# One core, one transformer layer with a mixture of experts: the last expert's products in banks of their own, weighted in halves, and the final norms of both tiles interleaved

## The chip, the cores and the metric

The kernel runs on one NeuronCore of a Trainium2 chip. TensorE (PE) multiplies, VectorE (DVE), ScalarE (ACT) and GpSimd (POOL) do the rest, SyncE (SP) issues the transfers. The metric is the device time of one launch in microseconds; lower is better. Each engine works through its own list of instructions in order, and the lists are tied together by semaphores that the kernel sets and waits for by name.

## The reference, cut to what matters

A first block (attention and a convolutional feed-forward part) and a second block (gated linear attention, pooling, and a mixture of 32 experts) run over 256 tokens of width 1024. The change lies in the end of the second block: the last expert, the sum over experts, and the last norm.

```python
def expert_block(args):
    xb, e = args
    return (jax.nn.silu(xb @ w_gate[e]) * (xb @ w_up[e])) @ w_down[e]
...
y_rows = y_rows * row_w[:, None].astype(y_rows.dtype)
out = jnp.zeros((T + 1, D), y_rows.dtype).at[row_token].add(y_rows)[:T]
...
x = x + hier_moe(h2, ...)
return rmsnorm_2(x, norm_f_g)      # x * rsqrt(mean(x*x) + eps) * g
```

All data are fp32, 256 tokens are two tiles of 128, an expert has an inner width of 256.

## The kernel before, in words

Weights come in 165 units of 1 MB (128 partitions by 2048 numbers), through a ring of 6 slots in SBUF; SP issues a unit as soon as `unit_used` says that its slot is free. The experts are worked on one after another, each with up to 64 tokens (`CH`); what does not fit in 64 goes to a second pass behind `If(total > 0)`, which the inputs here do not need. TensorE's list is skewed: in the turn of expert e (`experts(e)`) stand the gate and up products of expert e+1, the two transposes of expert e's activations (`expert_turn`, L1039), the scattering of expert e-1 (`scatter`, L1053) and the down products of expert e (`expert_down`, L1047).

- Down products: 4 fp32 products of 128x512 into banks 2 and 3 of PSUM (`psum[:, 2 + n, :]`), where every expert's stand. Each is two instructions in the trace, so there are 8 of them in a row. Their end adds 1 to `unit_used`.
- Weighting: ACT (`results`, L1421) waits for the down products, reads both banks (128x1024), multiplies each row by its routing weight and writes the rounded high part into `YH` (the tile `weighted`), `y_hi`. DVE (`results`: `tokens_of`, L2027, then `low_results`, L2031) writes for 64 partitions the rest that the rounding left, `y_lo`.
- Scattering: 4 products of 128x512 multiply `YH` by a 0/1 matrix (`W`, the tile `token_onehot`) and add into banks 4 to 7, two banks for each tile of tokens.
- The copy of the transposes: ACT's `turned` (L1164, 128x256) reads bank 1 and writes `AE`, which the down products read (`ae_ready`).

For the last expert (31) the turn has no products of a next one, so its order on TensorE is: transposes of 31, scattering of 30, down products of 31, and behind the turn the scattering of 31, which adds 1 to `y_done` for each tile. ACT does `results(30)`, `turned(31)`, `results(31)`.

The final norm goes tile by tile. DVE adds the tile's two banks to `X` (L2119, `final_x`); ACT squares and sums (L1145); DVE adds epsilon (L1566, 128x1); POOL takes the power -0.5 (L1499, 128x1); DVE multiplies `X` by the root and by the gain row `final` (L2124) and writes `HN`; SP stores the tile (L483). DVE's list holds all of tile 0 before any of tile 1:

```python
for tt in range(TT):
    dve.wait_ge(y_done, tt + 1)
    tt_op(X[:, tt, :], X[:, tt, :], psum[...], ADD).then_inc(final_x, 1)
    add_eps(11 + tt)
    roots_ready(11 + tt)
    dve.wait_ge(final_x, tt + 1)
    stt(HN[:, tt, :], X[:, tt, :], rstd[...], r_("final"), MUL, MUL).then_inc(out_ready, 1)
```

Between the last expert and the final norm each engine loads the number `total` and branches around the second pass.

Of the kernel before, what the change touches and what calls it, by code (L numbers as in the profile page):

```python
# [18 lines left out]
P = 128  # L19
S = 256  # L20
TT = S // P
# [34 lines left out]

NORM_PARTS = (2, 4, 2, 2, 2, 2, 2, 2, 2, 8, 2, 1, 1)
WHOLE = (2, 3, 4)
GROUP_SPANS = {2: slice(0, 512), 3: slice(512, 768), 4: slice(768, 1024)}


# [81 lines left out]
def build(nc, x_in, units_in, const_in, vec_in, rows_in, small_in, bias_in, out):  # L143
# [8 lines left out]
    with ctx:  # L152
# [3 lines left out]
        def sem(name):  # L156
            return ctx.enter_context(nc.semaphore(name))
# [161 lines left out]
        with nc.sbuf_tensor("tables_ahead", [P, A.at], fp32):  # L319
# [57 lines left out]
                  "more_lo", "more_scattered"))  # L377
        more_in, more_table, more_table_sb, more_added = map(
            sem, ("more_in", "more_table", "more_table_sb", "more_added"))
        out_ready, out_stored, final_x = sem("out_ready"), sem("out_stored"), sem("final_x")  # L380
        up_conv, pool_zero = sem("up_conv"), sem("pool_zero")
        dve_steps, act_steps, pool_steps = sem("dve_steps"), sem("act_steps"), sem("pool_steps")

# [61 lines left out]
        def _(sp):  # L445
# [32 lines left out]
                                     .rearrange("a p n -> p (a n)")).then_inc(more_loaded, 16)  # L478
                sp.nop()
            sp.nop()  # L480
            for tt in range(TT):
                sp.wait_ge(out_ready, tt + 1)
                sp.dma_start(out[tt], HN[:, tt, :]).then_inc(out_stored, 16)  # L483
            sp.wait_ge(out_stored, 16 * TT)


# [1 line left out]
        def _(pe):  # L488
# [575 lines left out]
            def experts(e, i=0):  # L1064

                if e < EXPERTS - 1:
                    pe.wait_ge(xw_lo, i * 2 + (e + 2))
                    pe.wait_ge(up_summed, i * 2 + (e + 1))
                    expert_up(0, XW[:, (e + 1) % 2], parts(gate_of(e + 1), i)).then_inc(unit_used, 1)
                    w = parts(gate_of(e + 1) + 1, i)  # L1070
                pe.wait_ge(at_ready, i * 2 + (e + 1))
                if e < EXPERTS - 1:
                    expert_up(1, XW[:, (e + 1) % 2], w, range(1))
                expert_turn().then_inc(at_tr, 1)
                if e < EXPERTS - 1:
                    expert_up(1, XW[:, (e + 1) % 2], w, range(1, KD)).then_inc(unit_used, 1)
                if e >= 1:
                    pe.wait_ge(y_lo, i * 2 + e)
                    for tt in range(TT):
                        last = scatter((e - 1) % 2, tt, 4 + 2 * tt, first=e == 1)  # L1080
                    last.then_inc(scattered, 1)
                w = unit(pe, down_of(e), i)
                pe.wait_ge(ae_ready, i * 2 + (e + 1))
                expert_down(w).then_inc(unit_used, 1)
# [9 lines left out]
                experts(4, i)  # L1094
                experts(5, i)
            experts(EXPERTS - 2)
            experts(EXPERTS - 1)
            pe.wait_ge(y_lo, EXPERTS)
            for tt in range(TT):
                scatter((EXPERTS - 1) % 2, tt, 4 + 2 * tt, final=True).then_inc(y_done, 1)  # L1100

            pe.wait_ge(total_ready, 1)
            total = pe.value_load(totali[0:1, 0:1], min_val=0, max_val=TASKS)
# [26 lines left out]
        def _(act):  # L1130
# [329 lines left out]
                experts(4, i)  # L1460
                experts(5, i)
            experts(EXPERTS - 2)
            experts(EXPERTS - 1)
            results(EXPERTS - 1)

            act.wait_ge(total_ready, 1)
            total = act.value_load(totali[0:1, 0:1], min_val=0, max_val=TASKS)
# [13 lines left out]
            act.nop()  # L1481
            for tt in range(TT):
                act.wait_ge(final_x, tt + 1)
                mean_squares(11 + tt, [X[:, tt, :]])


        @block.gpsimd
# [69 lines left out]
        def _(dve):  # L1557
# [517 lines left out]
                experts(4, i)  # L2075
                experts(5, i)
            experts(EXPERTS - 2)
            experts(EXPERTS - 1)
            results(EXPERTS - 1)

            dve.wait_ge(total_ready, 1)
            total = dve.value_load(totali[0:1, 0:1], min_val=0, max_val=TASKS)
# [34 lines left out]
            for tt in range(TT):  # L2117
                dve.wait_ge(y_done, tt + 1)
                tt_op(X[:, tt, :], X[:, tt, :], psum[:, 4 + 2 * tt:6 + 2 * tt, :].rearrange("p a b -> p (a b)"), ADD  # L2119
                      ).then_inc(final_x, 1)  # L2120
                add_eps(11 + tt)
                roots_ready(11 + tt)
                dve.wait_ge(final_x, tt + 1)
                stt(HN[:, tt, :], X[:, tt, :], rstd[:, 11 + tt, 0:1], r_("final"), MUL, MUL).then_inc(out_ready, 1)  # L2124


def constants():
# [136 lines left out]
```

## Time and profile before

| what | value |
|---|---|
| time, median of 3 runs | 869.8 us (869.47 to 870.5) |
| the profiled execution's own time | 868.98 us |
| its span, first to last instruction | 867.2 us |
| PE busy | 813.8 us, 94% of the span |
| DVE, ACT, POOL busy | 523.7, 451.1, 125.7 us |
| mean granted TensorE clock | 0.970 of full speed |
| moved by DMA | 181.44 MB, mean 209 GB/s |

The busy shares are means over the whole kernel. The change touches the last 25 us only, and there the slices of the page read 8 and 3 tenths for PE: TensorE is not what the end waits for. What matters is the chain of waits from the down products of the last but one expert to the last store.

### The profile page before, as it was taken

To read this page: it belongs to the slowest core of one execution; us is meant where nothing else is said; L and a number is where in the kernel's file an instruction comes from. 1 tells how busy PE (TensorE), PEld (TensorE's weight loads), DVE (VectorE), ACT (ScalarE), POOL (GpSimd) and SP (SyncE) were. 2 spreads that over 40 slices of the span, in tenths; PEclk is the share of its full clock that TensorE was granted. 3 is DMA by queue.
4 is the path that set the end of the run, shared out by engine and by line. 5 is a ranking of instruction groups with operands and counts; after the bars stand their busy time and mean duration, and the time that the engine had idled before them with its cause. 6 is when DMAs were issued, how large, how long until landed. Compare 5 with 4: busy or idle time off the path is not lost.

```text
span 867.2 us, 13148 instructions
## 1 busy us (share of the span) xinstructions
PE 813.8 (94%) x4792; PEld 660.9 (76%) x4792; DVE 523.7 (60%) x657; ACT 451.1 (52%) x590; POOL 125.7 (14%) x94
## 2 busy tenths in 40 slices
PE   6999999999999996998999989779999999999983
PEld 5888755999999994697899976467777777777761
DVE  3244435466556564655155565858888888888863
ACT  3243444454455443463244444267777777777741
POOL 0000001323422433103000000011111111111100
PEclk9999999999999998998799999889999999999996
DMA  9922221455555553152154543059999999999931
GB/s 368 386 98 97 97 97 48 150 192 194 193 172 179 185 190 103 43 190 102 50 195 146 194 149 143 0 197 351 369 353 378 373 352 353 380 359 373 373 146 50
DMA packets 25090, 181.44 MB, mean 209 GB/s; under 512 B 2784, under 2 KB 3040, under 8 KB 3296
## 3 DMA queue, kind: packets, MB, share of 16 engines
q1 hardware_dynamic: 25056, 180.97, 56.3%
q8 instruction: 24, 0.39, 0.2%
q14 instruction: 10, 0.08, 0.0%
HBM read 179.91 MB, written 1.05 MB: 209 GB/s over the span
## 4 chain that ended last, share of the span: by engine, by line
PE 86%; DVE 6%; ACT 3%; POOL 2%; issue 1%; DMA 1%; POOLq 0%; ACTq 0%; SPq 0%; DVEq 0%
PE psum L823 36%; PE psum L1032 15%; PE psum L1047 13%; PE psum L519 4%; PE psum L1053 3%; PE psum L618 3%; PE psum L527 2%; PE psum L577 1%; ACT junk L1145 1%; PE psum L1039 1%; PE psum L1024 1%; PE psum L942 1%; DVE arena L1764 1%; DVE ffn_w_low L438 1%; PE psum L940 1%
## 5 line engine op out<-in xcount | busy, mean ns | idle before, releaser
L438 DVE TENSOR_TENSOR ffn_w_low<-ring,ffn_w_high 128x2048 fp32r<-128x2048 f32 x57 | 135.0, 2372 | 123.4 <-ACT ffn_w_high L433 123.3
L433 ACT ACTIVATE ffn_w_high<-ring 128x2048 fp32r<-128x2048 f32 x57 | 109.2, 1918 | 144.1 <-PE psum L823 143.8
L823 PE MATMUL psum<-ht_high,ffn_w_high 128*128 128x256 f32 x576 | 164.3, 285 | 1.7 <-DVE ffn_w_low L438 1.1
L823 PE MATMUL psum<-ht_low,ffn_w_high 128*128 128x256 f32 x576 | 163.5, 284 | 0.0
L823 PE MATMUL psum<-ht_high,ffn_w_low 128*128 128x256 f32 x576 | 163.5, 284 | 0.0
L438 DVE TENSOR_TENSOR expert_w_low<-ring,expert_w_high 128x2048 fp32r<-128x2048 f32 x48 | 110.0, 2292 | 20.3 <-ACT expert_w_high L433 19.9
L1047 PE MATMUL psum<-ring,arena 128*128 128x512 f32 x256 | 116.7, 599 | 0.0
L823 PEld LDWEIGHTS psum<-ht_high,ffn_w_high 128*128 128x128 f32 x576 | 111.1, 193 | 3.2 <-issue 1.4
L1032 PE MATMUL psum<-expert_w_high,xw 128*128 128x256 f32 x384 | 106.1, 311 | 5.8 <-POOL xw L1543 3.9
L823 PEld LDWEIGHTS psum<-ht_low,ffn_w_high 128*128 128x128 f32 x576 | 111.1, 193 | 0.3
L823 PEld LDWEIGHTS psum<-ht_high,ffn_w_low 128*128 128x128 f32 x576 | 111.0, 193 | 0.0
L1032 PE MATMUL psum<-expert_w_low,xw 128*128 128x256 f32 x384 | 96.4, 286 | 0.0
L433 ACT ACTIVATE expert_w_high<-ring 128x2048 fp32r<-128x2048 f32 x48 | 91.4, 1904 | 3.5 <-PE psum L823 3.5
L1047 PEld LDWEIGHTS psum<-ring,arena 128*128 128x128 f32 x256 | 49.0, 192 | 49.8 <-issue 47.1
L1032 PEld LDWEIGHTS psum<-expert_w_high,xw 128*128 128x128 f32 x384 | 74.6, 194 | 12.3 <-POOL xw L1543 4.3
L1032 PEld LDWEIGHTS psum<-expert_w_low,xw 128*128 128x128 f32 x384 | 74.6, 194 | 3.6 <-issue 3.6
L1543 POOL TENSOR_TENSOR xw<-arena,xw 128x512 fp32r<-128x512 f32 x32 | 38.4, 1201 | 255.9 <-ACT xw L1164 255.9
L1164 ACT ACTIVATE arena<-psum 64x512 f32<-64x512 f32 (+6 forms) x96 | 46.2, 486 | 44.4 <-PE psum L1032 18.9
L1421 ACT ACTIVATE weighted<-psum,arena 128x1024 fp32r<-128x1024 f32 x32 | 35.8, 1119 | 59.1 <-PE psum L1047 59.1
L1499 POOL TENSOR_TENSOR rstd<-ms,neghalf 128x1 f32<-128x1 f32 (+3 forms) x19 | 14.1, 744 | 305.7 <-DVE ms L1566 305.7
L2031 DVE SCALAR_TENSOR_TENSOR weighted<-psum,arena,weighted 64x1024 fp32r<-64x1024 f32 x32 | 41.3, 1291 | 23.0 <-ACT weighted L1421 22.9
L1510 POOL TENSOR_TENSOR arena<-arena 128x512 f32<-128x512 f32 x11 | 31.9, 2901 | 127.2 <-ACT arena L1308 119.4
(296 smaller groups left out, 1405.4 us busy)
## 6 DMA issues: line engine op xcount, KB each, us to landing
ring<-units_in SPq DMA_DIRECT2D x165, 1024.0 KB, 5.9
rows<-rows_in SPq DMA_DIRECT2D x1, 1688.0 KB, 12.3
arena<-bias_in SPq DMA_DIRECT2D x1, 1536.0 KB, 15.6
small<-small_in SPq DMA_DIRECT2D x1, 1232.0 KB, 25.5
const<-const_in SPq DMA_DIRECT2D x1, 1073.0 KB, 23.0
X<-x_in SPq DMA_DIRECT2D x1, 1024.0 KB, 4.9
out<-HN SPq DMA_DIRECT2D x2, 512.0 KB, 2.6
vec<-vec_in SPq DMA_DIRECT2D x1, 113.5 KB, 4.4
```

Source lines behind the costliest of these rows:

```text
L433: nc.scalar.activation(parts_slot(n)[0], w, ACT.Copy).then_inc(hi_ready, 1)
L438: nc.vector.tensor_tensor(l, ring[:, n % RING, :], h.bitcast(fp32), SUB).then_inc(lo_ready, 1)
L519: last = mm(psum[:, bank, half * S:half * S + S], w[:, k * FF_CHUNK + half * P:k * FF_CHUNK + half * P + P], HT[:, k, :], start=k == 0, st ...
L618: last = mm(psum[:, 4 + 2 * tt + n, :], MIXT[:, 2 * j + kk, tt * P:(tt + 1) * P], w[:, kk * D + n * 512:kk * D + n * 512 + 512], start=j = ...
L823: last = mm(o, l[a], r[b], start=start and (a, b) == pairs[0], stop=stop and (a, b) == pairs[-1])
L1032: last = mm(psum[:, 0, g * D_EXP:(g + 1) * D_EXP], x[:, k, :], part[:, k * D_EXP:(k + 1) * D_EXP], start=k == 0 and part is w[0], stop=k = ...
L1047: last = mm(psum[:, 2 + n, :], AE[:, f, :], w[:, a:a + 512], start=f == 0, stop=f == 1)
L1164: return nc.scalar.activation(out_, in_, ACT.Copy)
L1421: return nc.scalar.activation(YH[:, par, :], psum[:, 2:4, :].rearrange("p a b -> p (a b)"), ACT.Copy, scale=TW[:, ds(weight, 1)])
L1510: nc.gpsimd.tensor_tensor(AF[:, c % 2], G[:, c % 2], up, MUL).then_inc(af_parts, 1)
L1543: nc.gpsimd.tensor_tensor(XW[:, e % 2, :, CH:], XS[:, :, ds(at, CH)], XW[:, e % 2, :, 0:CH].bitcast(fp32), SUB).then_inc(xw_lo, 1)
L2031: return stt(y, psum[CH:P, 2:4, :].rearrange("p a b -> p (a b)"), TW[CH:P, ds(column + EXPERTS, 1)], y.bitcast(fp32), MUL, SUB)
```

## The change

The last expert's turn is written out apart from `experts(e)` on the three engines.

- TensorE: down products of 31 go to banks 0 and 1 and stand right behind the transposes of 31, ahead of the scattering of 30. Each bank has a signal of its own (`last_down`). The scattering of 31 goes half by half: both tiles' products of columns 0 to 511, then both tiles' of columns 512 to 1023.
- ACT: `turned(31)` stands ahead of `results(30)`; the weighting of 31 is two instructions of 128x512 (`last_hi`) in place of one of 128x1024.
- DVE: the rest of 31 is two instructions of 64x512 (`last_lo`).
- Final norms: DVE adds both tiles first, then adds epsilon for tile 0, multiplies tile 1 by the gain row without its root (`gained`), adds epsilon for tile 1, and finishes tile 0 as before. ACT multiplies tile 1 by its root.

```diff
@@ TensorE
             experts(EXPERTS - 2)
-            experts(EXPERTS - 1)
-            pe.wait_ge(y_lo, EXPERTS)
+            last_e = EXPERTS - 1
+            pe.wait_ge(at_ready, EXPERTS)
+            expert_turn().then_inc(at_tr, 1)
+            w = unit(pe, down_of(last_e))
+            pe.wait_ge(ae_ready, EXPERTS)
+            for n in range(2):
+                for f in range(2):
+                    a = f * D + n * 512
+                    last = mm(psum[:, n, :], AE[:, f, :], w[:, a:a + 512], start=f == 0, stop=f == 1)
+                last.then_inc(last_down, 1)
+            pe.wait_ge(y_lo, EXPERTS - 1)
             for tt in range(TT):
-                scatter((EXPERTS - 1) % 2, tt, 4 + 2 * tt, final=True).then_inc(y_done, 1)
+                last = scatter((last_e - 1) % 2, tt, 4 + 2 * tt)
+            last.then_inc(scattered, 1)
+            for n in range(2):
+                pe.wait_ge(last_lo, n + 1)
+                for tt in range(TT):
+                    last = mm(psum[:, 4 + 2 * tt + n, :], W[:, last_e % 2, tt * P:(tt + 1) * P],
+                              YH[:, last_e % 2, n * 512:(n + 1) * 512], start=False, stop=True)
+                    if n == 1:
+                        last.then_inc(y_done, 1)
+            pe.nop().then_inc(unit_used, 1)
@@ ScalarE
-            experts(EXPERTS - 1)
-            results(EXPERTS - 1)
+            turned(EXPERTS - 1)
+            results(EXPERTS - 2)
+            act.wait_ge(scattered, EXPERTS - 2)
+            for n in range(2):
+                act.wait_ge(last_down, n + 1)
+                nc.scalar.activation(YH[:, (EXPERTS - 1) % 2, n * 512:(n + 1) * 512], psum[:, n, :], ACT.Copy,
+                                     scale=TW[:, 2 * EXPERTS - 1:2 * EXPERTS]).then_inc(last_hi, 1)
...
             for tt in range(TT):
                 act.wait_ge(final_x, tt + 1)
-                mean_squares(11 + tt, [X[:, tt, :]])
+                mean_squares(FINAL + tt, [X[:, tt, :]])
+            act.wait_ge(gained, 1)
+            act.wait_ge(rstd_ready, roots_before(FINAL + 2))
+            nc.scalar.activation(HN[:, 1, :], HN[:, 1, :], ACT.Copy, scale=rstd[:, FINAL + 1, 0:1]).then_inc(out_second, 1)
@@ VectorE
-            experts(EXPERTS - 1)
-            results(EXPERTS - 1)
+            results(EXPERTS - 2)
+            dve.wait_ge(scattered, EXPERTS - 2)
+            tokens_of((EXPERTS - 1) % 2, EXPERTS - 1)
+            for n in range(2):
+                dve.wait_ge(last_hi, n + 1)
+                y = YH[CH:P, (EXPERTS - 1) % 2, n * 512:(n + 1) * 512]
+                stt(y, psum[CH:P, n, :], TW[CH:P, 2 * EXPERTS - 1:2 * EXPERTS], y.bitcast(fp32), MUL, SUB
+                    ).then_inc(last_lo, 1)
...
-                add_eps(11 + tt)
-                roots_ready(11 + tt)
-                dve.wait_ge(final_x, tt + 1)
-                stt(HN[:, tt, :], X[:, tt, :], rstd[:, 11 + tt, 0:1], r_("final"), MUL, MUL).then_inc(out_ready, 1)
+            add_eps(FINAL)
+            dve.wait_ge(final_x, 2)
+            tt_op(HN[:, 1, :], X[:, 1, :], r_("final"), MUL).then_inc(gained, 1)
+            add_eps(FINAL + 1)
+            roots_ready(FINAL)
+            stt(HN[:, 0, :], X[:, 0, :], rstd[:, FINAL, 0:1], r_("final"), MUL, MUL).then_inc(out_first, 1)
```

SP waits for `out_first` and then for `out_second` in place of two counts of `out_ready`.

TensorE's list before, from the down products of expert 30 to the scattering of 31 (`ring` holds the down weights, `arena` the activations, `weighted` is `YH`):

```order
L1047 MATMUL psum<-ring,arena 128x512 [waits ae_ready,unit_loaded1]
L1047 MATMUL psum<-ring,arena 128x512 x3
L1039 MATMUL psum<-const,arena 128x64 [waits at_ready]
L1039 MATMUL psum<-const,arena 128x64
L1053 MATMUL psum<-weighted,token_onehot 128x512 [waits y_lo]
L1053 MATMUL psum<-weighted,token_onehot 128x512 x3
L1047 MATMUL psum<-ring,arena 128x512 [waits ae_ready,unit_loaded2]
L1047 MATMUL psum<-ring,arena 128x512 x3
L1053 MATMUL psum<-weighted,token_onehot 128x512 [waits y_lo]
L1053 MATMUL psum<-weighted,token_onehot 128x512 x3
```

The same place in the list of the changed kernel (its lines are numbered anew; L1051 and L1109 are the down products of 30 and of 31, L1057 and L1118 the scattering of 30 and of 31):

```order
L1051 MATMUL psum<-ring,arena 128x512 [waits ae_ready,unit_loaded1]
L1051 MATMUL psum<-ring,arena 128x512 x3
L1043 MATMUL psum<-const,arena 128x64 [waits at_ready]
L1043 MATMUL psum<-const,arena 128x64
L1109 MATMUL psum<-ring,arena 128x512 [waits ae_ready,unit_loaded2]
L1109 MATMUL psum<-ring,arena 128x512 x3
L1057 MATMUL psum<-weighted,token_onehot 128x512 [waits y_lo]
L1057 MATMUL psum<-weighted,token_onehot 128x512 x3
L1118 MATMUL psum<-weighted,token_onehot 128x512 [waits last_lo]
L1118 MATMUL psum<-weighted,token_onehot 128x512
L1118 MATMUL psum<-weighted,token_onehot 128x512 [waits last_lo]
L1118 MATMUL psum<-weighted,token_onehot 128x512
```

The down products of 31 moved ahead of the wait for `y_lo`, and the last scattering has two waits.

VectorE's list before, in the final norm, behind the branch:

```order
L2119 TENSOR_TENSOR X<-X,psum 128x1024 [waits y_done]
L1566 TENSOR_SCALAR ms<-ms 128x1 [waits squares_summed]
L2124 SCALAR_TENSOR_TENSOR HN<-X,rstd,rows 128x1024 [waits final_x,rstd_ready]
L2119 TENSOR_TENSOR X<-X,psum 128x1024 [waits y_done]
L1566 TENSOR_SCALAR ms<-ms 128x1 [waits squares_summed]
L2124 SCALAR_TENSOR_TENSOR HN<-X,rstd,rows 128x1024 [waits final_x,rstd_ready]
```

The same place after (`rows` is the tile of the gain row; L2159 is tile 1 by its gain, L2162 tile 0 by root and gain):

```order
L2155 TENSOR_TENSOR X<-X,psum 128x1024 [waits y_done] x2
L1596 TENSOR_SCALAR ms<-ms 128x1 [waits squares_summed]
L2159 TENSOR_TENSOR HN<-X,rows 128x1024 [waits final_x]
L1596 TENSOR_SCALAR ms<-ms 128x1 [waits squares_summed]
L2162 SCALAR_TENSOR_TENSOR HN<-X,rstd,rows 128x1024 [waits rstd_ready]
```

The second addition moved to the front, and a product of two SBUF tensors (`X` and `rows`) now stands between the two epsilons.

## Rows read from the trace of the kernel before

**Rows 1.** The page's first line.

```profile
span 867.2 us, 13148 instructions
```

**Rows 2.** Chain that ended last, 830 to 868 us: start us, us, what.

```profile
842.73 1.12 ACT weighted L1421
...
845.22 1.25 PE psum L1053 x4
...
851.58 1.12 ACT weighted L1421
...
852.73 1.30 DVE weighted L2031
...
854.08 0.75 PE psum L1053 x2
...
854.85 1.23 DVE X L2119
...
856.10 1.16 ACT junk L1145 x2
...
857.28 0.16 DVE ms L1566
...
857.52 0.54 POOL rstd L1499
```

**Rows 3.** Timeline, turns of experts 30 and 31: start us, us, engine, line, operation.

```profile
836.14 0.33 PE L1039 MATMUL psum<-const,arena 64*128 64x64 f32 x2
...
836.51 0.39 ACT L1164 ACTIVATE arena<-psum 128x256 f32<-128x256 f32 x1 [1.26 <-PE psum L1039]
...
839.10 3.60 PE L1047 MATMUL psum<-ring,arena 128*128 128x512 f32 x8
...
842.62 0.33 PE L1039 MATMUL psum<-const,arena 64*128 64x64 f32 x2
...
846.27 5.28 PE L1047 MATMUL psum<-ring,arena 128*128 128x512 f32 x8
```

**Rows 4.** Windows: stretch, length, busy of PE, PEld, DVE, ACT, POOL, clock, DMA.

```profile
843.00:846.20 3.20, 0.98 (x4) 0.85 (x5) 1.64 (x2) 1.12 (x2) 0.00 (x0) 1.00 0.00 0
846.30:849.60 3.30, 3.30 (x5) 1.31 (x4) 0.00 (x0) 0.00 (x0) 0.00 (x0) 0.50 0.00 0
```

**Rows 5.** Groups by line and form, whole run: xcount, busy us, mean ns, idle.

```profile
L1593 DVE TENSOR_TENSOR X<-X,arena 128x1024 f32<-128x1024 f32 x4 | 4.9, 1224 | 0.1
...
L1395 ACT ACTIVATE arena<-psum,vec 128x512 f32<-128x512 f32 x4 | 2.8, 691 | 11.5 <-PE psum L1024 11.5
...
L1153 ACT ACTIVATE HN<-X,rstd 128x1024 f32<-128x1024 f32 x4 | 4.6, 1147 | 5.1 <-POOL rstd L1499 5.1
```

**Rows 6.** Timeline of DVE and POOL at two earlier places.

```profile
179.67 2.29 DVE L438 TENSOR_TENSOR ffn_w_low<-ring,ffn_w_high 128x2048 fp32r<-128x2048 f32 x1
...
180.23 2.88 POOL L1510 TENSOR_TENSOR arena<-arena 128x512 f32<-128x512 f32 x1 [8.40 <-ACT arena L1308]
183.07 1.29 POOL L1511 TENSOR_TENSOR af_high<-arena 128x512 fp32r<-128x512 f32 x1
...
353.73 0.74 DVE L1576 TENSOR_SCALAR HN<-X,rstd 128x1024 f32<-128x1024 f32 x1
...
353.89 0.98 POOL L1499 TENSOR_TENSOR rstd<-ms,neghalf 128x1 f32<-128x1 f32 x1 [0.64 <-DVE ms L1566]
```

**Rows 7.** Timeline of the end, from the first store on.

```profile
859.40 4.78 SPq L483 DMA_DIRECT2D out<-HN  x2
...
862.54 1.28 DVE L2124 SCALAR_TENSOR_TENSOR HN<-X,rstd,rows 128x1024 f32<-128x1024 f32 x1 [0.66 <-POOL rstd L1499]
```

**Rows 8.** DMA issues of the page: KB each, us from issue to landing.

```profile
out<-HN SPq DMA_DIRECT2D x2, 512.0 KB, 2.6
```

**Rows 9.** Windows as in rows 4: the first store's data; an earlier stretch.

```profile
860.25:861.65 1.40, 0.00 (x0) 0.00 (x0) 0.25 (x1) 1.11 (x2) 0.00 (x0) 0.50 0.91 375
...
405.80:423.00 17.20, 16.13 (x53) 12.57 (x54) 1.06 (x4) 2.18 (x16) 2.43 (x4) 0.50 0.00 0
```

More of the change, by code:

```diff
@@ L58 @@
 WHOLE = (2, 3, 4)
+FINAL = 11
 GROUP_SPANS = {2: slice(0, 512), 3: slice(512, 768), 4: slice(768, 1024)}
@@ L379, in build @@
             sem, ("more_in", "more_table", "more_table_sb", "more_added"))
-        out_ready, out_stored, final_x = sem("out_ready"), sem("out_stored"), sem("final_x")
+        last_down, last_hi, last_lo = sem("last_down"), sem("last_hi"), sem("last_lo")
+        out_first, out_second, out_stored, final_x, gained = map(
+            sem, ("out_first", "out_second", "out_stored", "final_x", "gained"))
         up_conv, pool_zero = sem("up_conv"), sem("pool_zero")
@@ L480, in _ @@
             sp.nop()
-            for tt in range(TT):
-                sp.wait_ge(out_ready, tt + 1)
-                sp.dma_start(out[tt], HN[:, tt, :]).then_inc(out_stored, 16)
+            sp.wait_ge(out_first, 1)
+            sp.dma_start(out[0], HN[:, 0, :]).then_inc(out_stored, 16)
+            sp.wait_ge(out_second, 1)
+            sp.dma_start(out[1], HN[:, 1, :]).then_inc(out_stored, 16)
             sp.wait_ge(out_stored, 16 * TT)
```

## The prediction

> **What bounds the kernel now.** I read the chain of waits first, from the last instruction backwards. TensorE's share of the whole run (94%) says nothing about this change; the chain does. Up to the down products of expert 30 it runs through TensorE without a gap. From there it crosses engines one at a time [rows 2, 3]: transposes of 31 at 842.62, ACT's weighting of 30 at 842.73, scattering of 30 at 845.22, down products of 31 from 846.27, ACT's weighting of 31 at 851.58, DVE's rest at 852.73, scattering at 854.08, addition at 854.85, squares at 856.10, epsilon at 857.28, the root on POOL at 857.52. Then tile 1 goes through the same steps; its last product ends at 862.54 + 1.28 = 863.82 and is stored [rows 7]. So the last 24.6 us (842.62 to 867.2, [rows 1]) are a chain of latencies, and every microsecond taken out of it counts in full.
>
> Second, the clock. In 843.00 to 846.20 TensorE was busy for 0.98 us of 3.20 at full clock (2.4 GHz); in 846.30 to 849.60 it was granted half (1.2 GHz) [rows 4]. The last down products therefore took 5.28 us where those of expert 30 took 3.60 [rows 3]: 1.68 us lost.
>
> Third, the stores. The first is issued at 859.40 and its data move from 860.25 to 861.65, at 91% of the DMA engines [rows 7, 9]. A store takes 2.6 us from issue to landing [rows 8]. The second is issued at 863.82 + 0.02 = 863.84, lands at 866.44, and the span ends 0.76 later.
>
> **The change, part by part.** I walk the new order with the old durations.
>
> *Down products start earlier.* The transposes stay at 842.62. ACT's copy now comes right behind them: after 836.14 it started 0.37 later and took 0.39 [rows 3], so it ends at 843.38. A handoff costs 0.02 to 0.05 (852.73 + 1.30 = 854.03, then 854.08 [rows 2]); the down products start at 843.43 in place of 846.27: **2.84 us gained**. The ring slot is no obstacle: it was filled before, and no store or load runs here (0 GB/s in both windows of [rows 4]).
>
> *Full clock.* TensorE stands still only from 842.95 to 843.43. Before, it stood still until 845.22 ahead of the fall. I take full clock: **1.68 us gained**. First instruction to ACT's weighting was 3.63 (839.10 to 842.73, [rows 2, 3]), so bank 1 is ready at 843.43 + 3.63 = 847.06, and bank 0 half of 3.60 earlier, about 845.3.
>
> *ACT's moved weighting of 30* runs from 843.38 to about 844.5, DVE's rest of it to 845.8. Both are ahead of bank 0, and the scattering of 30 stands on TensorE behind the down products, which occupy it to about 846.9. It is hidden; if this cover were gone the price would be the 1.25 of that scattering [rows 2].
>
> *Halves.* No row shows an ACT weighting of 512 columns into `weighted`. It costs at least half of 1.12 = 0.56 and at most 1.12. The nearest row is ACT reading 512 columns of PSUM with a per-partition factor, 0.69 [rows 5]; I take that. DVE's half costs at least 0.65 and at most 1.30; an instruction on one column takes 0.16 [rows 2], so I take (1.30 + 0.16) / 2 = 0.73. Half 0 is long done (845.3 + 0.69 + 0.73 is under 847) and its two scatter products follow those of 30, until about 848.4. Half 1: 847.06 + 0.69 + 0.03 + 0.73 + 0.05 = 848.56. From ready banks to scattering that is 1.50 in place of 2.50 (851.58 to 854.08): **1.00 us gained**. The bounds give 1.29 to the whole 2.50.
>
> The Trainium skill (ScalarE: Activation LUTs, § What ACT_TABLE_LOAD costs) gives an ACTIVATE a fixed part of 186 ns, 93 ns more for a per-partition operand, and 0.833 ns for each element. By it a half costs 0.71, so that two halves cost more than a whole; it speaks against splitting as such, and would put the sum 0.02 later.
>
> *Last scattering.* The addition started 0.77 behind two products (854.08 to 854.85). Four take 1.25 and two 0.75 [rows 2], so one product is 0.25; only one now stands ahead of `y_done` for tile 0: 0.52, **0.25 us gained**. The addition of tile 0 starts at 849.08 in place of 854.85. Sum so far 5.77.
>
> *Branch.* DVE's load of `total` and its branch are in no row. Before, the addition started 2.12 behind the last weighting (852.73 to 854.85) and was released by TensorE, so the branch costs at most 2.12. Now the cover is 849.08 - 847.78 = 1.30. The exposed cost lies between 0 and 0.82; I take 0, since ACT and DVE never show a wait of their own there.
>
> *Final norms.* Additions at 849.08 and 850.31 (1.23 each) until 851.54. ACT's squares of tile 0 start 1.25 behind the addition and take 1.18 (854.85, 856.10, 857.28), so epsilon 0 can go at 851.54. POOL's root starts 0.24 later, 851.78. DVE's product of tile 1 by the gain, two SBUF tensors of 128x1024, costs 1.22 [rows 5]: 851.70 to 852.92. Epsilon 1 follows (ACT's second squares are done at 852.75).
>
> Here a wait appears that the old order did not have. At 180.23 POOL's product began under a DVE product of two SBUF tensors (179.67 to 181.96), and took 2.88 where its like took 1.29 alone: it ended 1.15 behind DVE's end, as if it had stood still. At 353.89 a root of 128x1 began under a DVE instruction (353.73 to 354.47) and took 0.98 in place of 0.54, ending 0.40 behind it [rows 2, 6]. So I let root 0 end at 852.92 + 0.40 = 853.32. DVE finishes tile 0 from 853.35 to 854.63, store at 854.65. Root 1 begins with it at 853.32, under another DVE instruction with two SBUF tensors, and ends at 854.63 + 0.40 = 855.03. ACT's product of tile 1 by its root costs 1.15 [rows 5]: 855.06 to 856.21, store at 856.23. From the first addition to the last store's issue: 7.15 in place of 8.99, **1.84 us gained**.
>
> No row has a root under a SCALAR_TENSOR_TENSOR of two SBUF tensors, as tile 0's last step is. The Trainium skill (GPSIMD Engine Reference, § 1. Specifications) says that POOL's SBUF interfaces are shared with VectorE, with contention for DVE instructions with two SBUF inputs; it would cover this one too. The rows agree for the two instructions that they show.
>
> *Stores.* The first one's data move 0.85 to 2.25 behind its issue, 855.50 to 856.90; the second's would start at 857.08. They do not meet. Cost 0.
>
> **Sum.** 5.77 + 1.84 = 7.61 us. All durations are of the profiled execution (868.98 us, span 867.2): it would take 861.4. The median of the runs is 869.8, 0.8 higher; against it I forecast **862.2 us**. A difference within 0.2% (1.7 us) could not be told from none.
>
> **The rivals.**
> - *POOL is not held up by DVE.* Root 0 ends at 852.32, tile 0 is stored at 854.38, root 1 ends at 853.70, tile 1 is stored at 854.90. Now the stores meet: the second's data could move at 855.75, but the first's occupy the engines to 856.63, so it lands 0.88 late, at 858.38 in place of 866.44: 8.06 gained, 861.7. If only the gain product holds POOL, the stores are issued at 854.65 and 855.06 and queue for 0.99: 7.79 gained, 862.0. Against it stand [rows 6]. Were there no queueing either, 8.94 would be gained (860.9), the lower bound.
> - *The clock falls all the same* on the last down products, after the 0.48 us gap. Price 1.68 again: 863.9. For it: it fell here before. Against it: TensorE idled 2.27 us then, and is busy right through now.
> - *The branch or the loading of code shows* on DVE, up to 0.82: 863.0.
> - *The change doesn't do what it says, or slower.* Both need one mechanism that gives back 7.6 us, and none lies in these 25 us. It would be the clock elsewhere: in 405.80 to 423.00 TensorE was busy 16.13 us at half clock [rows 9]. One more such stretch gives back 8.1 to 8.6, about 870.6, no change; slower by over 0.2% it becomes from 9.3 us more, a bit over one such stretch, and two would give 879. Against it: TensorE's list ahead of the last turn is untouched, and three runs lie within 1.0 us.
>
> **How the numbers follow.** Forecast 0.52, POOL not held 0.24, clock falls 0.10, branch 0.09, no gain 0.03, slower 0.02. The first four are all faster: 0.95. The likeliest four run from 860.9 to 863.9, and that is the range; the 0.8 us between profile and median lies inside it.
>
> **What would show it.** Down products of 31 (L1109) starting 0.4 to 0.5 us behind the transposes, 3.6 us long, at clock 1.00. Two ACT weightings of about 0.69. The first addition 6.5 us behind the transposes. POOL's two roots near 1.5 and 1.7 us long, ending 0.4 behind DVE's instructions: with 0.54 each the first rival is right. The stores 1.6 us apart rather than 0.5. The prediction is wrong if the windows show 0.50 on the last down products, if DVE's first addition waits for nothing that the profile shows, or if another stretch of the run changes its clock.

## The result and the profile after

The changed kernel was timed in three series, each beside runs of the kernel before on the same chip.

| series | after, median us | before, median us | ratio, 95% interval |
|---|---|---|---|
| first, 4 runs | 861.77 (860.22 to 863.23) | 869.83 (869.47 to 870.50) | 0.9895 (0.9864 to 0.9926) |
| second, 6 runs | 862.59 (860.08 to 867.20) | 870.55 (865.63 to 874.45) | 0.9914 (0.9881 to 0.9947) |
| third, 6 runs | 862.44 (859.95 to 866.88) | 870.62 (869.4 to 874.8) | 0.9894 (0.9860 to 0.9928) |

All 16 runs of the changed kernel have a median of 862.3 us; forecast were 862.2. Two measures of the gain differ. The medians lie 8.06, 7.96 and 8.18 us apart; the ratios, applied to 869.8, give 9.1, 7.5 and 9.2 us; 7.6 us were forecast. The 9.1 would be 860.7 us, just under the range's lower end of 860.9. Where the difference between 7.6 and what the totals say lies is one question of this document; the other is why the tail came out at 7.6 us although four of its terms were mis-sized.

The profiled execution after took 863.23 us, with a span of 861.5. The chain that ended last, from the down products of expert 30 on (start us, us, what):

```profile
841.13 3.43 PE psum L1051 x8
...
844.87 0.39 ACT arena L1186
845.26 0.14 issue
845.40 3.69 PE psum L1109 x8
...
849.11 0.70 ACT weighted L1490
...
849.83 0.77 DVE weighted L2114
...
850.64 0.75 PE psum L1118 x2
851.39 1.22 DVE X L2155
...
852.63 1.16 ACT junk L1167 x2
...
853.81 0.17 DVE ms L1596
...
854.04 1.45 POOL rstd L1529
```

It is the chain of [rows 2], shorter in two places. Between the transposes and the down products only ScalarE's copy of the transposes is left, where the weighting and the scattering of 30 stood; behind the down products each weighting instruction has half the columns. The timeline of the same execution, on the engines that matter:

```profile
844.50 0.33 PE L1043 MATMUL psum<-const,arena 64*128 64x64 f32 x2
...
845.40 3.67 PE L1109 MATMUL psum<-ring,arena 128*128 128x512 f32 x8 [0.57 <-ACT arena L1186]
...
851.37 2.35 DVE L2155 TENSOR_TENSOR X<-X,psum 128x1024 f32<-128x1024 f32 x2 [0.79 <-PE psum L1118]
...
853.88 1.22 DVE L2159 TENSOR_TENSOR HN<-X,rows 128x1024 f32<-128x1024 f32 x1
854.04 1.96 POOL L1529 TENSOR_TENSOR rstd<-ms,neghalf 128x1 f32<-128x1 f32 x2 [23.41 <-DVE ms L1596]
...
855.53 1.28 DVE L2162 SCALAR_TENSOR_TENSOR HN<-X,rstd,rows 128x1024 f32<-128x1024 f32 x1 [0.32 <-POOL rstd L1529]
856.10 1.15 ACT L1514 ACTIVATE HN<-HN,rstd 128x1024 f32<-128x1024 f32 x1 [1.08 <-POOL rstd L1529]
856.84 0.35 SPq L485 DMA_DIRECT2D out<-HN  x1
857.27 0.40 SPq L487 DMA_DIRECT2D out<-HN  x1
```

Read it against [rows 3, 7]. The down products of 31 took 3.67 us where they took 5.28. From the transposes to the first addition it is 851.37 - 844.50 = 6.87 us, before 854.85 - 842.62 = 12.23. The two roots together take 1.96: the first 1.45 in the chain above, under the gain product, the second the remaining 0.5. The stores are issued 0.43 apart. Three windows (columns as in [rows 4]) show the clock on the down products and the data of the stores:

```profile
845.40:849.10 3.70, 3.70 (x9) 1.78 (x10) 2.40 (x3) 1.54 (x2) 0.00 (x0) 1.00 0.00 0
857.70:859.00 1.30, 0.00 (x0) 0.00 (x0) 0.00 (x0) 0.00 (x0) 0.00 (x0) 0.50 1.03 425
859.00:860.35 1.35, 0.00 (x0) 0.00 (x0) 0.00 (x0) 0.00 (x0) 0.00 (x0) 0.50 0.89 364
```

Full clock, and the two stores' data back to back. In all, from the last transposes to the end: 861.5 - 844.5 = 17.0 us, before 867.2 - 842.6 = 24.6. That is the forecast 7.6, though not by the forecast terms, as the part on the prediction shows. But the transposes themselves came at 844.50 in place of 842.62, 1.9 us later, in a program whose list on TensorE is the same up to there. I call the stretch ahead of the last transposes the head, and what follows the tail.

### The profile page after: what moved, and what is told of

It reads as the page before. It is cut to its first block, busy times and chain, and to the rows that moved or that the text cites. A ratio compares the mean times of both kernels' runs of the same rounds, so it can differ in the third digit from the quotient of the medians.

```text
span 861.5 us, 13151 instructions
## 1 busy us (share of the span) xinstructions
PE 813.7 (94%) x4792; PEld 661.8 (77%) x4792; DVE 523.9 (61%) x658; ACT 452.6 (53%) x592; POOL 126.5 (15%) x94
## 3 DMA queue, kind: packets, MB, share of 16 engines
HBM read 179.91 MB, written 1.05 MB: 210 GB/s over the span
## 4 chain that ended last, share of the span: by engine, by line
PE 87%; DVE 6%; ACT 3%; POOL 2%; issue 1%; DMA 1%; POOLq 0%; ACTq 0%; SPq 0%; DVEq 0%
PE psum L827 37%; PE psum L1036 15%; PE psum L1051 12%; PE psum L523 4%; PE psum L622 3%; PE psum L1057 3%; PE psum L531 2%; PE psum L581 1%; ACT junk L1167 1%; PE psum L1043 1%; PE psum L1028 1%; PE psum L946 1%; DVE arena L1794 1%; DVE ffn_w_low L441 1%; PE psum L944 1%
## 5 line engine op out<-in xcount | busy, mean ns | idle before, releaser
L1051 PE MATMUL psum<-ring,arena 128*128 128x512 f32 x248 | 111.4, 592 | 0.0
L1051 PEld LDWEIGHTS psum<-ring,arena 128*128 128x128 f32 x248 | 46.9, 189 | 47.0 <-issue 44.5
```

Of the source, the lines that this page charges most:

```text
L1051: last = mm(psum[:, 2 + n, :], AE[:, f, :], w[:, a:a + 512], start=f == 0, stop=f == 1)
```

## The experiments

### e1 and e2: each half of the change alone

e1 keeps the last expert as before and takes the new norms; e2 the other way round. Both edits are shown against the changed kernel, cut to what matters.

```diff
 e1, TensorE (ScalarE and VectorE likewise: experts(EXPERTS - 1), results(EXPERTS - 1))
-            last_e = EXPERTS - 1
...
+            experts(EXPERTS - 1)
+            pe.wait_ge(y_lo, EXPERTS)
+            for tt in range(TT):
+                scatter((EXPERTS - 1) % 2, tt, 4 + 2 * tt, final=True).then_inc(y_done, 1)
 e2, VectorE
-            add_eps(FINAL)
-            dve.wait_ge(final_x, 2)
-            tt_op(HN[:, 1, :], X[:, 1, :], r_("final"), MUL).then_inc(gained, 1)
-            add_eps(FINAL + 1)
-            roots_ready(FINAL)
-            stt(HN[:, 0, :], X[:, 0, :], rstd[:, FINAL, 0:1], r_("final"), MUL, MUL).then_inc(out_first, 1)
+                add_eps(FINAL + tt)
+                roots_ready(FINAL + tt)
+                dve.wait_ge(final_x, tt + 1)
+                stt(HN[:, tt, :], X[:, tt, :], rstd[:, FINAL + tt, 0:1], r_("final"), MUL, MUL
+                    ).then_inc(out_first if tt == 0 else out_second, 1)
```

> The last expert as before; only the final norms are the new ones. Theory 1 (the whole gain lies behind the transposes of the last expert, and the stretch ahead of them varies from run to run alone): from the first addition to the landing of the last store 9.3 us in place of 11.6, so 2.3 us faster than before, about 867.5. The first root on GpSimd stands under the gain product and takes about 1.45 us, the second about 0.54. Rival, theory 2 (the changed program is also faster ahead of that place, by 0.5 to 1.5 us, since its code lies elsewhere): 866 to 867, though the tail in the profile is the same. If GpSimd were not held up at all, both roots would take 0.54.

> The last expert is the new one, the final norms are as before. Theory 1: from the transposes of the last expert to the first addition 6.9 us in place of 12.2, the tail behind it unchanged at 11.6, so 5.4 us faster than before, about 864.4; with e1 the two parts add up to 7.6 to 7.7. Theory 2: more than 5.4 by what the head gives, 863 to 864. The clock on the last down products is 1.00.

e1: 867.34 us median over 12 runs, ratio 0.9977 (0.9959 to 0.9996). e2: 865.34 over 6, ratio 0.9940 (0.9927 to 0.9954). Before in the same series: 869.93 over 17. In e1's timeline the addition starts at 855.05 and the span ends at 865.1: 10.1 us, where before it was 12.4 (867.2 - 854.85), so 2.3 gained. In e2's, the transposes and the first addition:

```profile
844.58 0.33 PE L1043 MATMUL psum<-const,arena 64*128 64x64 f32 x2
...
851.46 1.22 DVE L2152 TENSOR_TENSOR X<-X,psum 128x1024 f32<-128x1024 f32 x1 [0.79 <-PE psum L1118]
```

6.88 us in place of 12.23, so 5.35 gained; 2.3 + 5.35 is 7.6, the changed kernel's tail. The two parts do not touch each other. The medians give 2.6 and 4.6, the ratios 2.0 and 5.2 of 870: the same sizes, but with 95% intervals of 1.2 to 1.6 us to either side, which the tail does not have. Theory 1 stands for the tail. Of theory 2 nothing can be seen: the heads (842.8 and 844.6) are later than before's 842.6 and not earlier. That is one profile of each; the part on the prediction compares more.

### e3: the early order without the halves

```diff
-            for n in range(2):
-                pe.wait_ge(last_lo, n + 1)
-                for tt in range(TT):
+            pe.wait_ge(last_lo, 1)
+            for tt in range(TT):
+                for n in range(2):
...
+            nc.scalar.activation(YH[:, (EXPERTS - 1) % 2, :], psum[:, 0:2, :].rearrange("p a b -> p (a b)"), ACT.Copy,
+                                 scale=TW[:, 2 * EXPERTS - 1:2 * EXPERTS]).then_inc(last_hi, 1)
```

> As the changed kernel, but the last expert's results are weighted whole, by one ScalarE instruction over both banks and one VectorE instruction, and scattered tile by tile. If the halves are worth what their durations say, (1.11 - 0.69) + (1.29 - 0.76) + one product of 0.24 ahead of the first addition, this is 1.2 us slower than the changed kernel, about 6.4 us faster than before (863.4). Rival: two instructions cost their fixed part twice and the halves are worth nothing: within 0.3 us of the changed kernel.

863.26 us median over 6 runs, ratio 0.9922 (0.9897 to 0.9948). The profile is sharper: transposes at 844.14, and then

```profile
848.81 1.11 ACT L1489 ACTIVATE weighted<-psum,arena 128x1024 fp32r<-128x1024 f32 x1 [2.91 <-PE psum L1109]
849.96 1.29 DVE L2112 SCALAR_TENSOR_TENSOR weighted<-psum,arena,weighted 64x1024 fp32r<-64x1024 f32 x1 [2.35 <-ACT weighted L1489]
851.30 1.20 PE L1118 MATMUL psum<-weighted,token_onehot 128*128 128x512 f32 x4 [1.67 <-DVE weighted L2112]
852.08 2.35 DVE L2153 TENSOR_TENSOR X<-X,psum 128x1024 f32<-128x1024 f32 x2 [0.83 <-PE psum L1118]
```

The first addition is 7.94 us behind the transposes in place of 6.87: the halves are worth 1.07 us, 0.1 less than expected. From the last scattering's start to the addition the changed kernel takes 0.73 us and this one 0.78, so that the one product less ahead of the addition gave 0.05 and not the 0.24 expected; the part on the prediction shows what the addition waits for. The rival is dead: the two instructions of 0.69 us cost more together than the one of 1.11, but the first lies under the down products of the second half (847.45 to 848.14 in the changed kernel). The ScalarE half took 0.69 us, as the nearest row of before said. An estimate from the figures of the Trainium skill (ScalarE: Activation LUTs, § What ACT_TABLE_LOAD costs) is 0.71, and the trace agrees to 0.02.

### e4b: the clock alone

```diff
                 expert_turn().then_inc(at_tr, 1)
...
+                else:
+                    stay_busy(2, 0, X[:, 0, :])
```

> As before, with two idle products of 128x512 behind the transposes of the last expert, into bank 0, from the tile X; they fill 1.7 of the 2.3 us that TensorE waits there, and nothing is moved. If the lost clock is a cost of its own: granted clock 1.00 on the last down products, 3.6 us in place of 5.3, tail from the transposes to the end 22.9 us in place of 24.6, about 868.2. Rival: the clock falls all the same, or the idle products hold up the scattering behind them: tail 24.6 or more.

This is the kernel before with two products into bank 0 that nobody reads. The timeline of TensorE:

```profile
841.07 0.33 PE L1039 MATMUL psum<-const,arena 64*128 64x64 f32 x2
...
841.33 1.98 PE L494 MATMUL psum<-X,const 128*128 128x512 f32 x4
...
843.66 1.20 PE L1053 MATMUL psum<-weighted,token_onehot 128*128 128x512 f32 x4 [0.35 <-DVE weighted L2033]
844.70 3.60 PE L1047 MATMUL psum<-ring,arena 128*128 128x512 f32 x8
```

The last down products take 3.60 us in place of 5.28, nothing is delayed, and the tail is 864.0 - 841.07 = 22.9 us in place of 24.6. The lost clock was a cost of its own, 1.7 us. With the wait filled the clock stayed at full, which is as much as this run shows of why it fell. It is a part of the change's gain that could have been had without moving anything. In the total it drowns: 867.93 us over 12 runs (865.69 to 872.89), ratio 0.9985 (0.9957 to 1.0012).

### e5: a root under VectorE's last instruction

```diff
                 inverse_roots(11 + tt)
+                if tt == 0:
+                    nc.gpsimd.tensor_tensor(rstd[:, 12, 4:5], mse[:, 11, 0:1], neghalf[:, 0:1], ALU.pow)
```

> The changed kernel with one more root on GpSimd between the two that count, so that the second root of the norm starts some 0.5 us into VectorE's last instruction (SCALAR_TENSOR_TENSOR with two SBUF tensors) and not just ahead of it. If that instruction holds GpSimd up as the gain product did: the second root ends 0.4 us behind it, about 1.2 us long, and the second store is issued some 1.5 us later than before the edit. If it does not hold it up: 0.54 us long, and the store 0.5 us later.

```profile
858.12 1.22 DVE L2161 TENSOR_TENSOR HN<-X,rows 128x1024 f32<-128x1024 f32 x1
858.29 1.45 POOL L1529 TENSOR_TENSOR rstd<-ms,neghalf 128x1 f32<-128x1 f32 x1 [23.40 <-DVE ms L1598]
...
859.71 0.54 POOL L1585 TENSOR_TENSOR rstd<-ms,neghalf 128x1 f32<-128x1 f32 x1
859.77 1.29 DVE L2164 SCALAR_TENSOR_TENSOR HN<-X,rstd,rows 128x1024 f32<-128x1024 f32 x1 [0.32 <-POOL rstd L1529]
860.21 1.24 POOL L1529 TENSOR_TENSOR rstd<-ms,neghalf 128x1 f32<-128x1 f32 x1
```

Three roots on the same amount of data, 128x1, in the one execution that this kernel had. The one that begins 0.06 us ahead of VectorE's instruction takes 0.54; the two that begin under one take 1.45 and 1.24 and end 0.40 and 0.39 behind it (858.12 + 1.22 = 859.34 and 859.74; 859.77 + 1.29 = 861.06 and 861.45). So GpSimd is held by either kind of instruction, and what saves it is to have begun. The Trainium skill (GPSIMD Engine Reference, § 1. Specifications) names contention with VectorE instructions with two SBUF inputs; the trace agrees, for TENSOR_TENSOR and SCALAR_TENSOR_TENSOR both. Two inputs in SBUF are not the whole condition, though. The root at 353.89 [rows 6] was held in the same way under a TENSOR_SCALAR with one wide tensor, `X`, while another root of before began under an instruction that takes one of its wide inputs from PSUM, and was not held:

```profile
136.03 1.27 DVE L1590 SCALAR_TENSOR_TENSOR arena<-psum,rstd,rows 128x1024 f32<-128x1024 f32 x1
...
136.19 0.55 POOL L1499 TENSOR_TENSOR rstd<-ms,neghalf 128x1 f32<-128x1 f32 x1 [0.60 <-DVE ms L1566]
```

In e5 the second store is issued 862.72 - 855.62 = 7.10 us behind the first addition, where the changed kernel has 5.90: 1.2 later, 1.5 expected. The stores are now 1.63 apart, the 1.6 of the prediction, and do not meet, so that the tail is only 0.4 longer (866.1 - 848.74 = 17.4). The execution took 867.97 us because its head was 848.74.

### e6: stores in quarters

```diff
+            add_eps(FINAL)
+            roots_ready(FINAL)
+            half(0, 0)
+            add_eps(FINAL + 1)
+            half(0, 1)
+            roots_ready(FINAL + 1)
+            half(1, 0)
+            half(1, 1)
...
+                    sp.wait_ge(out_first, 2 * tt + n + 1)
+                    sp.dma_start(out[tt][:, c], HN[:, tt, c]).then_inc(out_stored, 16)
```

> The changed kernel with another end: no gain product and no ScalarE factor; VectorE finishes tile 0 and then tile 1 in halves of 512 columns, each stored at once (four stores of 256 KB), the epsilon of tile 1 between the halves of tile 0. The first root stands under nothing and takes 0.54 us. Counted from the first addition: halves end at 4.0, 4.8, 5.5 and 6.1 us if the second root is free, 0.5 later if the half of tile 0 holds it; the last store has only a quarter of the data to move, 1.9 us from issue to landing. End at 8.8 to 9.3 us in place of 10.1, so 0.8 to 1.3 us faster than the changed kernel, about 861.2. Rival: stores of 2 KB rows cost so much more each that the last lands as late as before.

861.96 us over 6 runs (859.24 to 862.34), ratio 0.9898 (0.9870 to 0.9926). The tail is 16.6 us, 0.4 less than the changed kernel's; 0.8 to 1.3 was expected.

```profile
853.40 0.54 POOL L1527 TENSOR_TENSOR rstd<-ms,neghalf 128x1 f32<-128x1 f32 x1 [23.47 <-DVE ms L1594]
...
854.71 0.74 DVE L2159 SCALAR_TENSOR_TENSOR HN<-X,rstd,rows 128x512 f32<-128x512 f32 x1
854.75 2.99 SPq L488 DMA_DIRECT2D out<-HN  x4
854.87 0.98 POOL L1527 TENSOR_TENSOR rstd<-ms,neghalf 128x1 f32<-128x1 f32 x1 [0.93 <-DVE ms L1594]
```

The first root is free at 0.54, the second is held by half an instruction and takes 0.98. The rest of the miss is the last store. Its data are all but through at 859.00, but in the window behind that one of the 16 DMA engines still works (a share of 0.08; 27 GB/s over 0.45 us are 12 KB, six packets of 2 KB). Fifteen of the store's 16 parts have landed by 859.39, the last at 859.95:

```profile
858.95:859.40 0.45, 0.00 (x0) 0.00 (x0) 0.00 (x0) 0.00 (x0) 0.00 (x0) 0.50 0.08 27
```

### e7: the clock far from the change

If the head decides the spread, the place to look is the longest low stretch, the 17 us around 405.80 to 423.00 [rows 9]. It begins within a wait of 3.3 us on TensorE, which in the changed kernel ends so:

```profile
408.38 0.77 PE L944 MATMUL psum<-arena 128*128 128x128 f32 x2 [3.26 <-DVE HT L1869]
```

e7 is the changed kernel with three products in that wait, into a bank that is free:

```diff
+            stay_busy(3, 7, X[:, 0, :])
             pe.wait_ge(st_sb, 2)
             pe.wait_ge(states_ready, 3)
```

> The changed kernel with three idle products of 128x512 in the wait of 3.3 us that TensorE has ahead of the small products of the gated linear attention, some 440 us before the last expert. Those small products ran at half clock for 17.1 us in every profile so far (16.1 us of TensorE busy). Theory (the clock's low stretches far from the change set how long the program takes to reach the last expert, and so the spread of 3 to 9 us between runs): with the wait filled the low stretch there is shorter or gone, up to 8 us are saved, total 854 to 860, and the tail behind the last transposes stays at 17.0 us. Rival: the small products do not hold the clock whatever precedes them; the low stretch stays near 17 us and the total near 862.

854.63 us median over 6 runs (854.37 to 861.29), ratio 0.9819 (0.9783 to 0.9855): 7.8 us faster than the changed kernel in the same series, and by its median the fastest kernel of this study. Timeline and window of the place:

```profile
403.45 2.84 PE L498 MATMUL psum<-X,const 128*128 128x512 f32 x6
...
406.79 0.46 PE L945 MATMUL psum<-arena 128*128 128x128 f32 x2 [0.49 <-DVE HT L1870]
407.18 0.48 PE L947 MATMUL psum<-HT,arena 64*128 64x128 f32 x2
```

```profile
406.00:424.00 18.00, 17.51 (x121) 15.31 (x121) 3.85 (x8) 5.72 (x19) 3.56 (x4) 1.00 0.14 47
```

The small products take 0.46 a pair in place of 0.77 in the changed kernel, the clock stays at 1.00, and the transposes of the last expert come at 852.5 - 17.0 = 835.5. The tail is unchanged. Two of the six runs took 857.32 and 861.29, with a mean clock of 0.980 and 0.977 where the others had 0.984.

### e8: the changed kernel again

> The changed kernel a third time, to pin the size: 7.6 us behind the last transposes says a ratio of 0.9912 to before, with an interval that holds it. Rival: 9.1 us, a ratio of 0.9895 as in the first runs, with 0.9912 left out. The tail in the profile is 17.0 us again, wherever the transposes come.

The second series had the same kernel:

> The changed kernel itself, once more beside the others. Theory 1 (the gain is 7.6 us behind the transposes of the last expert, and what the runs show beyond it or short of it is how long the program took to get there): 17.0 us from those transposes to the end as in its first profile, and a median of 861 to 863, near 862.3. Rival: the first runs were right and the change is worth 8.1 to 9.1 us: a median of 861.7 or less with an interval that leaves out 7.6. In the profile the transposes come at 842.6 if TensorE's clock first rises at 10.0 us, and at 844.5 if at 12.0.

The tails are 17.0 us both times (861.2 with the transposes at 844.20; 859.9 with 842.90). The head follows the clock's first rise, as the expectation said: the record of the granted clock begins at full at 11.86 us in the first of these two, at 10.28 in the other, at 12.01 in the changed kernel's first profile (head 844.50) and at 9.97 in before's (842.62). The intervals of all three series hold both 0.9895 and 0.9912, so neither size can be excluded by totals.

### e9: e6 and e7 together

> e6 and e7 in one kernel: the quarter stores and the filled wait ahead of the small products. Independent gains would give 854.6 - 0.4 = 854.2. In e6 the last store took 2.56 us from issue to landing, the others about 2.0; if that was one late packet of that execution, the tail here is 16.1 us (last store 2.0 us); if it belongs to the fourth store, it is 16.6 again. Rival: the two together are no faster than e7 alone.

858.62 us median over 6 runs, from 852.52 to 863.12, ratio 0.9854 (0.9813 to 0.9895). The tail is 16.6 us as in e6, so the slow last store belongs to it and was no accident of one execution. But in the profiled execution the fill did not hold the clock: the windows say

```profile
405.80:410.60 4.80, 4.31 (x19) 2.40 (x17) 1.87 (x5) 0.00 (x0) 3.20 (x3) 1.00 0.00 0
410.80:424.20 13.40, 13.40 (x50) 11.16 (x50) 1.04 (x4) 2.18 (x16) 1.65 (x1) 0.50 0.01 2
```

The small products began at full clock at 407.88, 0.49 us behind the fill as in e7's profile, and lost it 2.8 us later under way, although TensorE had been busy without a gap since they began. What differs from e7's execution is not known. The gain of e7 is not there in every execution: four of e7's six runs had a mean clock of 0.984, three of e9's six had 0.983 to 0.985. The best run of all, 852.52, is one of e9's; whether e9's typical run is faster than e7's stays open with six runs each.

## Why the prediction was right and where it was wrong

Most of the mechanism was right: the down products started early and at full clock, the halves cost what was forecast, and the first root was held. That the tail's gain came out at the forecast 7.6 us was luck: the experts' part gave 5.36 us and not 5.77, the norms' part 2.27 and not 1.84, and the two errors cancel. That the median over all runs, 862.3, met the 862.2 is in part luck too, since before's median over its 60 runs is 870.1 and not 869.8. The first series' ratio, 9.1 us, lies outside the range. By its steps:

- *Down products earlier, full clock.* Right. 845.40 - 844.50 = 0.90 us behind the transposes, 0.81 forecast: between ScalarE's end and the first product lie 0.14 us where 0.05 was taken from VectorE's handoff. Clock 1.00; e4b priced it at 1.7 alone.
- *Halves.* Sizes right (0.69 and 0.76 for 0.69 and 0.73).
- *Last scattering.* Right for TensorE. The one product ahead of the signal for tile 0 ends 0.50 us after its start, and the signal (`y_done`) comes at 851.16, 0.52 behind the start as forecast.
- *Branch.* Wrong: it was put at 0, and 0.2 us show. These are the products ahead of the addition in the changed kernel, and the two in before:

```profile
850.64 0.50 PE L1118 MATMUL psum<-weighted,token_onehot 128*128 128x512 f32 x1 [0.19 <-DVE weighted L2114]
```

```profile
854.08 0.74 PE L1053 MATMUL psum<-weighted,token_onehot 128*128 128x512 f32 x2 [2.53 <-DVE weighted L2031]
```

In before the addition starts 0.03 us behind their end, and 0.02 behind the semaphore event in the trace. In the changed kernel it starts at 851.37, 0.23 us behind the end and 0.22 behind the event. The profile names TensorE as what released it, but the signal had long come. VectorE's addition starts 1.54 to 1.55 us behind the start of its last weighting in all eight profiles with the halves, and the signal comes at 1.32 to 1.33; in the four without them the signal comes at 2.10 and the addition starts at 2.12. Between the two VectorE's list holds nothing but the load of `total` and the branch. So they and what follows them take about 1.5 us from the start of that weighting, and with the shorter weighting they are no longer covered. Which part of them takes it no run shows. This is the rival "the branch shows, up to 0.82", at 0.2. With ScalarE's handoff (0.09), the time from the first down product to the weighting (849.11 - 845.40 = 3.71 where 3.63 was taken) and the halves (0.03), it makes the 0.41 by which the experts' part fell short.
- *First root held by the gain product.* Right: 1.45 us, 1.54 forecast. One reading behind it was too wide: of the two VectorE instructions in [rows 6] that were taken to agree with "two SBUF inputs", the TENSOR_SCALAR has one wide input.
- *Second root held by VectorE's last instruction.* Wrong as to time, right as to rule. I let both start together and gave VectorE the way. The root came 0.06 us earlier and was through in 0.54; e5 shows that half a microsecond later it would have been held. The last store is issued 857.27 - 851.37 = 5.90 us behind the first addition in place of 7.15: 1.25 better than forecast.
- *Stores do not meet.* Wrong, by the step before: they were issued 0.43 us apart, and the second landed 860.70 - 857.27 = 3.4 us behind its issue in place of 2.6: 0.8 lost where the cost was put at 0. Both errors together made the norms' part 2.27 in place of 1.84. This is the first rival's case that only the gain product holds GpSimd, whose part behind the first addition was 2.0.
- *How the numbers follow.* Here is the step that failed for the total. The range was built from the tail's unknown costs, and the head was taken as fixed, since "three runs lie within 1.0 us"; its spread between runs got no term. Three runs were too few to see it: 56 later runs of the kernel before go from 865.6 to 874.8, in groups (five at 865.6 to 866.1 at a mean clock of 0.974, 40 at 869.1 to 870.8 at 0.970, eleven at 872.7 to 874.8 at 0.961 to 0.964). The tail is the same to 0.02 us in every profile of one kernel; the head of the changed kernel was 844.50, 844.20 and 842.90.

What moves the head is the granted clock. First, when it rises after the start; the chain's first products, of before, of the changed kernel's first profile and of its third (e8), in this order:

```profile
5.89 4.85 PE psum L494 x6
```

```profile
5.93 5.49 PE psum L498 x6
```

```profile
5.86 5.03 PE psum L498 x6
```

The same six products take 4.85, 5.49 and 5.03 us, and the transposes come at 842.62, 844.50 and 842.90; in e2, also with 5.49, at 844.58. The Trainium skill (TensorE: Matmul & The Clock Gate, § Part 1) says that the point of the rise varies, by 0.5 us to either side, since what decides it runs free of the kernel's start. The traces agree that it varies, but by more: full clock begins between 9.09 and 12.08 us in the twelve profiles. Why, no run shows. Eight of the profiles have equally long low stretches between the rise and the last transposes (before, the changed kernel three times, e1, e2, e3 and e6), and in these the head lies 832.3 to 832.7 us behind the rise, in before (832.65) as in the changed kernel (832.49, 832.34, 832.62). Second, which stretches are low: e5's profile, the slowest, has low windows that the first profile of the changed kernel does not have. The same place in e5 and in the changed kernel:

```profile
514.40:517.60 3.20, 3.01 (x7) 2.46 (x8) 2.24 (x2) 0.00 (x0) 0.00 (x0) 0.50 0.62 261
```

```profile
514.40:517.60 3.20, 2.86 (x13) 2.40 (x14) 2.40 (x2) 0.00 (x0) 0.00 (x0) 1.00 0.67 282
```

What a low stretch costs is shown by e7: taking the longest away gave 7.8 us by the medians, and 6.8 in the profile if the head is counted from the rise (835.52 - 9.82 = 825.7 where the eight have about 832.5). My rival "the clock elsewhere" had the kind right and the price a little high (8.1 to 8.6 for one such stretch, as if everything in it took twice as long; the small products took 0.77 in place of 0.46, 1.7 times), and I used it only for a loss.

What stays open: whether the 0.4 to 0.6 us by which the medians exceed 7.6, and the 1.5 of the first and the third ratio, are chance. No part of them is in the tail, and counted from the rise the heads of the changed kernel agree with the one of before to 0.3 us; TensorE's list ahead of the last turn is the same. For the third ratio the groups say much: five of before's eleven runs in that series lie near 874.5 us, and one of the changed kernel's six at 866.9. Without these, among before's runs at a mean clock of 0.970 and the changed kernel's at 0.974 to 0.975, the means are 869.8 and 861.9, 7.9 apart. Chance is the simplest reading, with spreads like these, but for what is left it was argued and not shown.

## What to carry to other kernels

Price an end that is a chain of latencies from the rows of its own chain: it came out to 0.02 us from run to run, and moving work out of it pays in full. Ask of each engine whether something of its own, a branch for instance, ends later than the signal that the profile names, once what covered it is shortened. Forecast the total with a range that also holds what the rest of the program does between runs, which has nothing to do with the change; where the granted clock falls in waits, look at the length of the low stretches before anything else, since one filled wait of 3 us gave about as much here as the whole change. On VectorE, put an instruction with two SBUF operands just behind GpSimd's small one and not ahead of it: in e5 a start of the root 0.06 us ahead of it or 0.44 behind made it 0.54 or 1.24 us long.

## What was not expected of the hardware

- Small fp32 products did not bring the clock back in 17 us in which TensorE was busy for 16.1 at 1.2 GHz, and held 2.4 GHz when they started with it, in e7's profile for all their length; in e9's they lost it 2.8 us after they began, without a gap.
- A store of 256 KB as the last of four took about as long from issue to landing as one of 512 KB (2.6 us), because the part of one DMA engine landed 0.6 us behind the other fifteen, in both kernels that had it. The median of the four was 2.0.
- A GpSimd instruction on one column that begins under a VectorE instruction with two SBUF operands ends 0.4 us behind it, with 0.58 us of it left (e6), 0.84 (e5's last root) or 1.05 (the first roots). The same 0.4 stands behind the TENSOR_SCALAR of [rows 6], and nothing of it under one that reads PSUM.
- The first instruction behind a branch on VectorE came 1.5 us after the start of the instruction ahead of it, though that one took 0.76 and the signal waited for had come at 1.33.
